# Sums paced over the middle feed-forward steps, x rows first, waits per tile at changes of form

## The reference

```python
def ffn_sublayer(s, mods, w1, w3, w2, lw, lb):
    shift, scale, gate = mods
    h = layer_norm(s) * (1.0 + scale) + shift
    return layer_norm(ALPHA * s + 0.5 * gate * ((silu(h @ w1) * (h @ w3)) @ w2), lw, lb)
...
mods_x = split(silu(c) @ ada_w[l] + ada_b[l], 9)       # shift, scale, gate of three sub-layers
mods_c = split(silu(c_ctx) @ ada_w[l] + ada_b[l], 9)
x, ctx = ffn_sublayer(x, ...), ffn_sublayer(ctx, ...)
hx, hc = modulate(x, ...), modulate(ctx, ...)          # q, k, v, gates, ... = hx @ w_in, hc @ w_in
y = (sigmoid(g_ret) * retention(q, k, v) + sigmoid(g_na) * neighbourhood(nq, nk, nv)
     + sigmoid(g_fou) * fourier(fu)) @ w_o
x = layer_norm(ALPHA * x + g_x * y_x, ...)             # ctx alike, but not in the last layer
x, ctx = ffn_sublayer(x, ...), ffn_sublayer(ctx, ...)
```

## Time and profile before

| | us |
|---|---|
| median of three runs | 2739.52 (2738.04 to 2742.15) |
| the profiled execution's own time | 2739.35 |
| its span, first to last instruction | 2737.5 |
| TensorE busy | 2502.3 (91%) |
| VectorE busy | 1597.6 (58%) |
| ScalarE busy | 929.7 (34%) |

### The profile page before, as it was taken

How to read it: one execution, slowest core, us unless ns; L and a number is a source line. 1 busy time by engine, 2 the same in 40 slices (tenths; PEclk the granted TensorE clock), 3 DMA queues, 4 the chain that set the end, 5 groups by cost and what they waited for, 6 DMA issues and landing times.

```text
span 2737.5 us, 33189 instructions
## 1 busy us (share of the span) xinstructions
PE 2502.3 (91%) x13338; PEld 2146.3 (78%) x13338; DVE 1597.6 (58%) x2130; ACT 929.7 (34%) x1353; POOL 124.7 (5%) x163
## 2 busy tenths in 40 slices
PE   6999999898999999879999999999998898995898
PEld 6877888776766778768778887779887775995796
DVE  4566568545545544375665775666774644565555
ACT  2422345331114312243223562214552213333343
POOL 2000001000000000020000010000110001001000
PEclk9999999998999999899999999999999998997999
DMA  8544555341212334344545564445553232663663
GB/s 249 154 161 165 169 184 182 110 139 31 83 52 71 119 109 145 106 142 145 165 158 177 177 212 143 152 146 193 177 177 108 63 100 78 200 208 123 189 198 129
DMA packets 468492, 396.40 MB, mean 145 GB/s; under 512 B 36212, under 2 KB 420468, under 8 KB 468084
## 3 DMA queue, kind: packets, MB, share of 16 engines
q1 hardware_dynamic: 456672, 386.98, 44.5%
q10 hardware_dynamic: 11668, 7.30, 0.9%
HBM read 393.06 MB, written 1.17 MB: 144 GB/s over the span
## 4 chain that ended last, share of the span: by engine, by line
PE 77%; DVE 11%; ACT 5%; issue 3%; DMA 2%; POOL 0%; ACTq 0%; SPq 0%; POOLq 0%; DVEq 0%
PE ps L1327 22%; PE ps L1328 22%; PE ps L1329 22%; DVE wl L835 2%; ACT wh L503 2%; DVE acc L850 2%; ACT tB L521 2%; PE ps L1584 1%; PE ps L1575 1%; PE ps L1596 1%; PE ps L1524 1%; PE ps L1352 1%; DVE st L893 1%; DMA araw<-in_ada_w 1%; PE ps L1359 1%
## 5 line engine op out<-in xcount | busy, mean ns | idle before, releaser
L835 DVE TENSOR_TENSOR wl<-raw,wh 128x1024 fp32r<-128x1024 f32 x568 | 692.7, 1221 | 846.9 <-ACT wh L503 846.7
L503 ACT ACTIVATE wh<-raw 128x1024 fp32r<-128x1024 f32 x568 | 601.8, 1061 | 1440.1 <-PE ps L1329 1407.9
L1327 PE MATMUL ps<-hh,wh 128*128 128x256 f32 (+1 forms) x2672 | 893.0, 334 | 55.3 <-DVE hl L928 41.3
L1328 PE MATMUL ps<-hl,wh 128*128 128x256 f32 (+1 forms) x2672 | 883.6, 331 | 0.0
L1329 PE MATMUL ps<-hh,wl 128*128 128x256 f32 (+1 forms) x2672 | 882.4, 330 | 0.0
L1327 PEld LDWEIGHTS ps<-hh,wh 128*128 128x128 f32 x2672 | 517.1, 194 | 104.3 <-DVE hl L928 42.9
L1328 PEld LDWEIGHTS ps<-hl,wh 128*128 128x128 f32 x2672 | 516.9, 193 | 45.3 <-issue 1.2
L1329 PEld LDWEIGHTS ps<-hh,wl 128*128 128x128 f32 x2672 | 516.1, 193 | 44.9
L850 DVE SCALAR_TENSOR_TENSOR acc<-araw,c,acc 128x1024 f32<-128x1024 f32 x210 | 259.0, 1280 | 27.8 <-DMA araw<-in_ada_w 26.2
L1327 PE MATMUL ps<-wh,stage_h_f 128*128 128x512 f32 x616 | 240.8, 391 | 2.0 <-DVE stage_l_f L980 2.0
L1328 PE MATMUL ps<-wl,stage_h_f 128*128 128x512 f32 x616 | 239.8, 389 | 0.0
(11 more groups left out here) (160 smaller groups left out, 2440.7 us busy)
## 6 DMA issues: line engine op xcount, KB each, us to landing
raw<-in_ffa_w SPq DMA_DIRECT2D x204, 512.0 KB, 3.8
raw<-in_ffb_w SPq DMA_DIRECT2D x168, 512.0 KB, 4.2
raw<-in_mix_w_in SPq DMA_DIRECT2D x140, 512.0 KB, 4.0
araw<-in_ada_w SPq DMA_DIRECT2D x136, 512.0 KB, 4.8
raw<-in_mix_w_o SPq DMA_DIRECT2D x24, 512.0 KB, 3.5
raw<-in_ret_w_out SPq DMA_DIRECT2D x16, 512.0 KB, 4.3
raw<-in_na_fou_w_out SPq DMA_DIRECT2D x16, 512.0 KB, 4.0
raw<-in_ada_w SPq DMA_DIRECT2D x8, 512.0 KB, 5.1
```

The lines of the kernel that those rows point to most:

```text
L503: A.activation(wh[:, s, :], raw[:, s, :], ACT.Copy).then_inc(w_rounded, 1)
L835: V.tensor_tensor(wl[:, s, :], raw[:, s, :], f(wh[:, s, :]), ALU.subtract).then_inc(w_split, 1)
L1327: T.matmul(out, a[0], b[0], start=start, stop=False)
L1328: T.matmul(out, a[0], b[1], start=False, stop=False)
```

## The change

- FFN_ADA does the 24 sums in three groups of four steps, two a step, with a step without sums before each use. LAST_ADA does one a step; the use moves from step 5 to step 9.
- ret_in does all 16 rows for x first, then the ctx rows one by one (32 units in layer 0 instead of 28, 20 in layer 1 instead of 16). Each rope matmul follows a unit from n = 10 on and takes the next bank in turn (`ret_slots`). The last copies of a stage are waited for per tile or per group (`rv_banks`, `nv_banks`, fourier).
- At boundaries where both streams are worked on, residual(2) stands before the first splits, residual(3) at step 0, and the later parts of the ctx chain at other steps.
- `down` does its last four units tile by tile in the last half also where that half is ctx (before only in the last two sub-layers).
- In the merge the one-column matmuls move behind the third unit at mm = 3 and behind the whole loop for the second; `down` waits for modulation values later.

```diff
-FFN_ADA = (0,) * HEAD + (2, 1, 2, 1, 2) * 3 + (0,) * HEAD
-LAST_ADA = (2, 1, 2, 1, 2) + (0,) * (KF - 5)
+FFN_ADA = (0,) * HEAD + (2, 2, 2, 2, 0) * 3 + (0,) * HEAD
+LAST_ADA = (1,) * KD + (0,) * (KF - KD)
...
 def ret_steps(l):
-    first = [(r, 0, SEQ) for r in (*range(KD), *range(12, 16))] + [(r, 0, TOK) for r in range(8, 12)]
-    if l == DEPTH - 1:
-        return first
-    return first + [(r, SEQ, TOK) for r in (*range(KD), *range(12, 16))]
+    first = [(r, 0, SEQ) for r in (*range(KD), *range(12, 16), *range(8, 12))]
+    return first + [(r, SEQ, TOK) for r in ((*range(KD), *range(12, 16)) if l < DEPTH - 1 else ())] + [(r, SEQ, TOK) for r in range(8, 12)]
+
+def ret_slots(l):
+    out, j = [], 0
+    for n, (r, lo, hi) in enumerate(ret_steps(l)):
+        out.append(("unit", n, r, lo, hi))
+        if KD + 2 <= n < KD + 10:
+            out.append(("rope", j, ret_steps(l)[n - 2][0] - KD))
+            j += 1
+    return out
...
 # scalar, ffn: the ctx tiles
-                        if q == 4:
-                            normalise(i, 2)
-                        if q == 5:
-                            normalise(i, 3)
-                            modulate(i, 2)
-                        if q == 6:
-                            modulate(i, 3)
+                    elif htiles(i) == NT and q in (3, 5):
+                        normalise(i, 2 + q // 4)
...
                     A.activation(sgf[:, j, lo:hi], ps[:, B[2 * j], lo:hi], ACT.Sigmoid).then_inc(ff_sig, 1)
+                    if i and htiles(i) == NT and q in (3, 5):
+                        modulate(i, 2 + q // 4)
                     rounded(v + 5)
...
 # scalar, mixer: normalise(2), modulate(2), normalise(3), modulate(3) at j = 6, 7, 8, 12 (before 7, 9, 9, 11)
...
 # vector
             def begin(i, u):
                 if both(i - 1):
+                    residual(i, 2)
                     for j in range(RING):
                         split(u + j)
...
 # vector, ffn: residual 3 at q = 0, front at 1 and 3, rest at 4 and 6 (before residual 0, 1, front 2, 3, rest 6, 7)
+                    if i and htiles(i) == NT and q == 6:
+                        rest(i, 3)
...
 # vector, mixer: residual 3 at n = 0, front at 2 and 5, rest at 10 and 14 (before residual 0, 2, front 4, 6, rest 11, 12)
...
 # tensor, down
-                for q in range(2 * n):
+                    pe.wait_ge(mods_ready, 2 * (i + 1) + 1)
+                total = 2 * n if both(i) else n
+                for q in range(total - TAIL):
...
                         if i % 3 == 1:
                             pe.wait_ge(g_sum, 5 + 40 * (l + 1))
+                            pe.wait_ge(mods_ready, 2 * (i + 2))
...
+                t0 = LT if both(i) else 0
+                for t in range(t0, t0 + LT):
+                    for q in range(total - TAIL, total):
+                        if t == t0:
+                            staged(q)
+                        ins = product(q, t, last=q == total - 1)
...
 # tensor, mixer
+                for m, slot in enumerate(slots):
+                    if m >= 4:
+                        before = slots[m - 4]
+                        if before[0] == "unit":
+                            pe.wait_ge(in_copied, c0 + 3 + before[1] + 1)
+                        else:
+                            pe.wait_ge(rope_done, 8 * l + before[1] + 1)
...
+                token_form(AT["rv", l], KD, D, rv_tile, (1, 2, 0, 3), rv_banks)
...
-                pe.wait_ge(in_copied, c0 + 3 + RET[l] + 4)
                 pe.wait_ge(r_fin, r0[l] + len(r_items[l]))
                 for t in range(len(f_items[l]) + 1):
                     if t < len(f_items[l]):
                         gr, s = f_items[l][t]
+                        pe.wait_ge(in_copied, c0 + 3 + RET[l] + gr + 1)
...
                     form_a(v, 0, src, N)
-                    if mm == 3:
-                        ada_mods(i, 0, 6)
-                    if mm == 7:
-                        ada_mods(i, 1, 7)
...
                     form_a(v + 2, 2, src, N)
+                    if mm == 3:
+                        ada_mods(i, 0, 6)
...
-                pe.wait_ge(mods_ready, 2 * (i + 2))
+                pe.wait_ge(g_sig, 24 * l + 3 * (KD - 1) + 5)
+                ada_mods(i, 1, 2)
                 down(i, AT["wo", l], KD)
```

More of the change, by code:

```diff
@@ L260, in y_tiles @@
         def y_tiles(i):
-            return sum(not both(j) for j in range(i))
+            return i
         OUT_BANKS = ((6, 0, 2, 4), (6, 0, 2, 4), (2, 4, 6, 0), (6, 0, 2, 4), (6, 0), (2, 4))
@@ L297, in trunk @@
         in0 = [0, RET[0] + 12]
-        rope_rows = [[(n, r - KD) for n, (r, a, b) in enumerate(ret_steps(l)) if r >= KD and a == 0] for l in range(DEPTH)]
-        X_UNITS = 12
-        def rope_at(l, n):
-            late = [max(m + 1, X_UNITS) for m, k in rope_rows[l]]
-            return [j for j in range(8) if late[j] == n]
+        X_UNITS = 16
         r_items = [[(h, s) for h in range(RH) for s in range(2 if l < DEPTH - 1 else 1)] for l in range(DEPTH)]
@@ L1014, in ffn @@
                     elif htiles(i) == NT:
-                        if q in (0, 1):
-                            residual(i, q + 2)
-                        if q in (2, 3):
-                            front(i, q)
-                        if q in (6, 7):
-                            rest(i, q - 4)
+                        if q == 0:
+                            residual(i, 3)
+                        if q in (1, 3):
+                            front(i, 2 + q // 2)
+                        if q == 4:
+                            rest(i, 2)
                     if q >= len(steps) - TAIL:
@@ L1187, in mixer @@
                     dve.wait_ge(unit_done, u + n + 1)
[L1188 to L1192 removed]
+                    V.tensor_copy(dst, ps[:, bank, lo:hi]).then_inc(in_copied, 1)
                 for p in range(4):
@@ L1282, in mixer @@
                     if mm == 7:
-                        next_mods(i, 1, 7)
+                        next_mods(i, 1, 2)
                     else:
@@ L1486, in token_form @@
                     ready(u + k)
-                    for t in range(NT):
+                    for t in order:
+                        if k == 0:
+                            banks_free(t)
                         ins = product(k, t)
@@ L1616, in inputs @@
                         form_a(u + j, j, src, n)
-                def rope(j):
-                    m, k = rope_rows[l][j]
-                    pe.wait_ge(in_copied, c0 + 3 + m + 1)
-                    if j >= 2:
-                        pe.wait_ge(rope_done, 8 * l + j - 1)
-                    T.matmul(ps[:, 4 + j % 2, 0:SEQ], swap[:], kq[:, k, 0:SEQ], start=True, stop=True).then_inc(rope_mm, 1)
                 u = AT["ret_in", l]
-                B = in_banks(i)
+                B, slots = in_banks(i), ret_slots(l)
@@ L1628, in mixer @@
                 pe.wait_ge(h_lo, pre0(i) + LT)
-                for n, (r, lo, hi) in enumerate(ret_steps(l)):
+                for m, slot in enumerate(slots):
[5 more added lines that the diff above has]
+                            pe.wait_ge(rope_done, 8 * l + before[1] + 1)
+                    if slot[0] == "rope":
+                        _, j, k = slot
+                        pe.wait_ge(in_copied, c0 + 3 + KD + j + 1)
+                        T.matmul(ps[:, B[m % 4], 0:SEQ], swap[:], kq[:, k, 0:SEQ], start=True, stop=True).then_inc(rope_mm, 1)
+                        continue
+                    _, n, r, lo, hi = slot
```

102 lines of the change are left out of this document (44 added, 58 removed).

## The result

The changed kernel takes 2575.98 us (median of 4 runs, 2572.8 to 2580.36), against 2738.78 for the kernel before on the same chip: ratio 0.9404, 95% interval [0.9388, 0.9421]. I had forecast 2605 us and a range of 2588 to 2637. The direction was right, but the gain is 163 us instead of 134, and the range missed it by 12.

A forecast was written before the change was run, and what follows sets the result against it. TensorE was taken as the bound, standing 235 us in short waits, nearly all on VectorE, with slow clock behind stops. Terms 49 + 32 + 14 + 30 + 10 - 1 = 134 us off 2739.4 gave 2605 us, range 2588 to 2637.

The forecast's parts named there:

- A: Feed-forwards: modulation sums end two steps before use, so waits for acc (39.8 us) and slow clock (9.5) go; 49 us, bounds 39.8-52.
- D: Merge: moved one-column matmuls end the acc and modT waits; those matmuls keep their 6.4 us; 30 us gained, bounds 27 to 36.
- B: Entry of the two mixers: waits 26 and clock 13 us go, less narrow units 2.5 and new waits 4.8; 32 us.
- C: Waits per tile at nv's first tile and the Fourier transforms: 10 + 3.6 = 14 us gained, bounds 9 to 16.
- E: Context tiles in second and third feed-forward: waits and clock 14.8 us, of which 4.4 stay; 10 us gained, bounds 0-15.
- F: Down's last four units tile by tile in the context half: costs 1 us, 6 if the cover fails.
- (1): Rival: VectorE's queue takes the wait over, five entries waiting 5 us each plus clock; time 2632 us; chance 0.12.
- (2): Rival: the clock does not come back, shorter stops, thin matmuls and transposes still lower it; 2640 us; chance 0.08.
- (3): Rival: weight loads bound the narrow units at the mixers' entries, making it slower; time from 2740 us; chance 0.02.
- (4): Rival: rows are reordered but the same event ends last, so little changes; time 2735 to 2740 us; chance 0.02.

## Why the prediction was too careful

**A, 49 us: the mechanism was right, the clock mis-sized.** The sum gave 9.5 us to the clock behind the waits; transposes and gate matmuls alone got back 13.8 (9.9 and 3.9) where the part was undone, and the part measured 55.7 undone and 62.3 alone, above its upper bound of 52 both times. I had priced three of the six bursts of transposes, and the gate matmuls only within the last feed-forward's 1.7. For the shorter stops I wrote that the clock stayed at 1.00 behind five of six; that reading was wrong. In the kernel before, the gate matmuls of feed-forward 3 behind a wait of 2.41 us ran slow too:

```profile
1718.55:1723.38 4.83, 4.83 (x8) 0.65 0.53 175
```

The same eight take 3.0 us with no stop. And it changes from execution to execution: with the sums undone all three bursts of transposes behind waits of 2.5 us ran at 0.50 to 0.52, where in the kernel before one of three was slow. So a stop of 2.5 us has a price here, and one execution doesn't give it.

**D, 30 us: here the step failed.** "The 32 one-column matmuls stay, 6.4 us. They ran at 0.54": I saw the slow clock in the earlier trace rows, took the length as given, and argued only over the unit behind them. A duration read at half clock is no property of the work. With the wait gone they take 3.9 and 3.6 us in layer 0 and 1.84 twice in layer 1, 9.6 us less in all. The part measured 36.3 alone and 47.8 undone, the latter above its upper bound of 36 even without the 7.5 us of the last attention. The other question was whether these matmuls hold the clock. The Trainium skill says of transposes that they don't count as busy in the same way ("TensorE: Matmul & The Clock Gate", Part 4: PE-mode transpose). Whether that carries over to one-column matmuls I left open. It does: the doubled burst shows 0.50 with TensorE busy throughout. But in layer 0 the units behind lose 1.5 and 1.6, not 2.9. In layer 1 the first burst is over before the clock falls, and only the unit behind the second, with a wait of 1.28 us between, loses 1.7.

**B, C and E, 56 us: right as a group, 62 measured with F.** B's new waits for kq are 0.59 and 0.16 us per mixer, not 1.4 and 1.0, so my chain of VectorE and ScalarE around unit 15 was 1.7 too pessimistic each time. E's 1.7 and 2.7 us that stay are 1.06 and 1.07. C's second stage of the Fourier transforms waits for fA (3.6), as said. No run takes B, C and E apart, so errors in them may cancel.

**F, -1 us: right in the sum, wrong as a part.** It costs 0.8 at mixer 0, where `down` now waits 2.8 and 3.9 us for stage_l_m; I had named one such wait. But as the cover of the early residual, which I had put in E, it is worth 20.7; the pair is worth 11.

**Waits without a term:** 13.3 us less, 5.4 more. These 7.9 us net are half of what the forecast missed in waits; tB and jd moved with the new entries, and what in them did it isn't shown.

**Rivals.** None came: no new wait for VectorE is longer than 3.9 us (1), the clock is 0.975 (2), the narrow units of the mixers' entries run with no wait above 0.6 (3), and the chains moved (4). The low end of the range, 2588, left out even my own bounds, since the range was drawn around things that could go wrong: the upper bounds of A, B, D, C and E add up to 52 + 37 + 36 + 16 + 15 = 156, so 2583 at best. Even that is 7 us above the result, and what is missing is mostly clock: A's bound held 12.2 us of it, where transposes and gate matmuls alone came to 13.8, and D's held nothing for the length of the bursts.

## What to carry to other kernels

When a stall ahead of a stretch goes, price everything behind it at full clock, thin matmuls and transposes too: read each duration together with the granted clock it was taken at, and halve it where that was 0.5 (here 16 transposes took 3.3 us at 0.50 and 1.7 at 1.00). Read the clock behind the same stop in more than one execution. Edits that look free may be the cover of another; undo them one by one before you call them so. Starting a helper's work earlier can put it beside work that it slows, so look at what runs on the neighbouring engine in the new place.

## What the runs showed of the hardware

A burst of one-column matmuls lets the clock fall though TensorE is counted as busy: 32 in a row (3.88 us) ran at 0.92, the next 32 at 0.50 (6.65 us); 16 at a time (1.7 us) between wide units left it at 1.00. Where a wait of 1.28 us followed the 16, the unit behind ran at 0.61 to 0.65 in the profiles of six kernels and at 1.00 in two.

GpSimd's operations on 128x1 columns took 0.21, 0.57, 0.19 and 0.24 us with VectorE idle, and 1.08, 1.41, 0.68 and 1.08 beside VectorE's splits, which read two tensors from SBUF. VectorE being busy isn't enough: the last two of the tile before took 0.19 and 0.24 us in the changed kernel while VectorE took statistics, which read one tensor; the first two had taken 1.14 and 1.58 beside passes that read two. The Trainium skill ("GPSIMD Engine Reference", Specifications) says that the two engines share their SBUF interfaces and that VectorE instructions with two SBUF inputs contend for them; the trace agrees, 4.25 us against 1.21 for the four.
